# Right half of the up rows as one dense product, left half gathered, down rows first

## The reference

```python
    top_s, pos = lax.top_k(cand, PEER_TOPK)
    idx = jnp.take_along_axis(cand_idx, pos, axis=-1)      # 16 of 16384 experts, for each token and each of 8 heads
    gate = jax.nn.softmax(top_s, axis=-1)
    ...
        u_sel = jnp.take(expert_down, ib, axis=0)           # 128 rows of 2048 for each token
        act = jnp.einsum('tkd,td->tk', u_sel, hb)
        w = gb * jax.nn.gelu(act, approximate=False)
        v_sel = jnp.take(expert_up, ib, axis=0)             # 128 other rows for each token
        return jnp.einsum('tk,tkd->td', w, v_sel)
```

## Time and profile before

| | us |
|---|---|
| median of three runs | 3584.25 (3583.43 to 3586.36) |
| span of the profiled execution | 3584.6 |
| busy in it: PE / POOL / DVE / ACT | 3250.7 / 2185.8 / 1757.3 / 1332.6 |

### The profile page before, as it was taken

One profiled execution on the slowest core, in us unless ns is written; L12 is line 12 of the kernel. 1 busy time (PEld: TensorE's weight loads), 2 busy tenths in 40 slices (PEclk: granted clock), 3 DMA queues, 4 the chain that ended last, 5 costly groups with the idle time before them and its releaser, 6 DMA issues.

```text
span 3584.6 us, 38956 instructions
## 1 busy us (share of the span) xinstructions
PE 3250.7 (91%) x13696; PEld 2311.8 (64%) x13696; DVE 1757.3 (49%) x2582; ACT 1332.6 (37%) x2038; POOL 2185.8 (61%) x1216
## 2 busy tenths in 40 slices
PE   9999999996787788777777789999999999999998
PEld 7888878874343334222322338888888888888887
DVE  8998264238566447544744452222232233335444
ACT  6776576442111011000100014444444444445553
POOL 2021767876445444455455537887788778878665
PEclk9999999998999999999999999999999999999999
DMA  7455545659999999999999985555555455555444
GB/s 230 138 150 139 169 147 164 210 195 367 419 419 420 421 419 421 421 419 421 421 416 422 418 344 194 176 176 170 167 175 174 168 168 176 175 187 174 150 144 170
DMA packets 232766, 936.79 MB, mean 261 GB/s; under 512 B 28177, under 2 KB 31249, under 8 KB 166033
## 3 DMA queue, kind: packets, MB, share of 16 engines
q0 software_dynamic: 76288, 538.74, 36.4%
q1 hardware_dynamic: 152848, 391.96, 33.7%
q10 hardware_dynamic: 3456, 3.77, 0.3%
HBM read 927.04 MB, written 2.10 MB: 259 GB/s over the span
## 4 chain that ended last, share of the span: by engine, by line
PE 65%; DMA 25%; DVE 5%; POOL 2%; issue 1%; DVEq 1%; ACT 1%; ACTq 0%; POOLq 0%
PE products L675 41%; DMA arena<-peer_up_in,arena 22%; PE products L2190 8%; PE products L1545 6%; DMA arena<-peer_down_in,arena 3%; DVE arena L2145 1%; POOL arena L2136 1%; PE products L1215 1%; PE products L2752 1%; PE products L1321 1%; PE products L2714 1%; PE products L1238 1%; POOL weights_low L1480 1%; DVE weights_low L634 1%; DVE arena L2171 0%
## 5 line engine op out<-in xcount | busy, mean ns | idle before, releaser
L634 POOL TENSOR_TENSOR weights_low<-arena,weights_high 128x1024 fp32r<-128x1024 f32 x484 | 1187.5, 2462 | 370.4 <-ACT weights_high L622 324.4
L2190 PE MATMUL products<-arena 128*128 128x512 f32 x1984 | 937.0, 619 | 289.5 <-DMA arena<-peer_up_in,arena 235.5
L622 ACT ACTIVATE weights_high<-arena 128x1024 fp32r<-128x1024 f32 x604 | 637.8, 1059 | 981.0 <-PE products L675 949.3
L675 PE MATMUL products<-weights_high,input_high 128*128 128x512 f32 x2416 | 985.4, 408 | 14.9 <-DVE weights_low L634 13.3
L675 PE MATMUL products<-weights_low,input_high 128*128 128x512 f32 x2416 | 947.2, 392 | 0.0
L675 PE MATMUL products<-weights_high,input_low 128*128 128x512 f32 x2416 | 944.5, 391 | 0.0
L2190 PEld LDWEIGHTS products<-arena 128*128 128x128 f32 x1984 | 370.5, 195 | 838.1 <-issue 416.6
L2145 DVE SCALAR_TENSOR_TENSOR arena<-arena 128x2048 f32<-128x2048 f32 x256 | 585.7, 2292 | 520.6 <-DMA arena<-peer_down_in,arena 520.2
L2136 POOL DMA_INDIRECT arena<-peer_up_in,arena x256 | 391.4, 1529 | 522.8 <-PE products L2190 499.9
L675 PEld LDWEIGHTS products<-weights_high,input_high 128*128 128x128 f32 x2416 | 455.6, 189 | 111.2 <-DVE weights_low L634 15.7
L675 PEld LDWEIGHTS products<-weights_low,input_high 128*128 128x128 f32 x2416 | 454.6, 188 | 98.2
(11 more groups left out here) (369 smaller groups left out, 3088.4 us busy)
## 6 DMA issues: line engine op xcount, KB each, us to landing
arena<-dsa_in SPq DMA_DIRECT2D x320, 512.0 KB, 3.5
arena<-w_in_in SPq DMA_DIRECT2D x128, 512.0 KB, 3.8
arena<-mla_wide_in SPq DMA_DIRECT2D x88, 512.0 KB, 3.5
arena<-w_attn_o_in SPq DMA_DIRECT2D x32, 512.0 KB, 3.8
arena<-w_out_in SPq DMA_DIRECT2D x32, 512.0 KB, 4.7
arena<-peer_w_query_in SPq DMA_DIRECT2D x32, 512.0 KB, 10.2
arena<-dsa_w_out_in SPq DMA_DIRECT2D x32, 512.0 KB, 3.7
arena<-glu_w_b_in SPq DMA_DIRECT2D x16, 512.0 KB, 3.8
```

Of the source, the lines that this page charges most:

```text
L622: nc.scalar.activation(w_hi[:, u % RING, :, at], ring[:, u % RING, :, at], ACT.Copy).then_inc(hi_made, 1)
L634: ops.tensor_tensor(w_lo[:, u % RING, :, at], ring[:, u % RING, :, at], w_hi[:, u % RING, :, at].bitcast(F32), op=ALU.subtract).then_inc(l ...
L675: mm = nc.tensor.matmul(PS[:, bank(b) + t, 0:width], x[:, x0 + n, at], y, start=n == 0 and m == 0, stop=n == len(parts) * PK - 1 and m == 2)
L2190: mm = nc.tensor.matmul(PS[:, SUM_BANKS[q]], diag[:, d % ROWS], row[:, q * NC:(q + 1) * NC], start=h % 2 == 0 and n == 0, stop=bool(last))
```

## The change

- All 256 down rows come first, in eight buffers (`load_down`, `dot_row`). In heads 1 to 12 three of 16 (n = 4, 8, 12: `helped`) are multiplied by POOL in place (`multiply_row`) and summed by ACT (`sum_row`, now another function); DVE dots the rest. POOL multiplies row j - 4 behind the gather of row j.
- Up rows are split by columns into two tensors in main memory, `up_left` and `up_right`, 16384 x 1024 each. The left half is still gathered, 256 gathers of 0.52 MB (`load_half`, six buffers), and added to X by DVE with the weight as a scalar (`add_half`).
- The right half is read whole, 128 chunks of 128 x 1024 (`load_dense` on SP, four buffers), and multiplied on PE by a dense matrix of weights: `spread[t][i2, i1, token]` is the weight of expert i1 x 128 + i2 for a token, zero where it isn't chosen. It is made for four tokens a group, 64 groups: POOL compares i2 with 0..127 for the 128 chosen experts of each token (`mark_keys`), DVE does so with i1 and multiplies by the weight (`mark_weights`), PE multiplies the two one-hot matrices (`spread_group`), ACT copies the result (`take_group`). Groups 0 to 28 stand among the last two heads' rows, the other 35 behind them. `dense_rows` waits for all 64.
- The input of the second block is turned in another order (left half of both tiles, then right half), and SP fills the first weight tiles as buffers come free. The half products between the last rows are gone. Masks and rope tables move behind the middle of the dense product.

```diff
+DOWNS = ROW_HEADS * TOPK
+HALVES = [(4 * r + 2 * t + p, n) for r in range(PEER_H // 2) for p in range(2) for n in range(TOPK) for t in range(NT)]
+HALF_BUFS = 6
+DENSE_BUFS = 4
+GROUP = 4
+LAST_OF_TILE = (13, 15)
+HELPED = (4, 8, 12)
+def helped(h, n):
+    return 1 <= h <= 12 and n in HELPED
+def group_of(h, n):
+    g = (h - LAST_OF_TILE[0]) * TOPK + n - GROUP_SLOT
+    return g if 0 <= g and h < ROW_HEADS - 1 else None
...
+        def multiply_row(pool, j):
+            down_here(pool, j)
+            t = j // TOPK // 2 % 2
+            nc.gpsimd.tensor_tensor(down_place(j), down_place(j), h2[:, t], op=ALU.mult).then_inc(down_multiplied, 1)
+        def sum_row(act, h, n):
...
+            nc.scalar.activation(down_place(j), down_place(j), ACT.Copy, accum_out=acts[:, h % 2, n:n + 1])\
+                .then_inc(down_summed, 1)
...
+        def add_half(dve, m):
...
+            nc.vector.scalar_tensor_tensor(out=X[:, t, 0:HALF], in0=halves[m % HALF_BUFS], scalar=weights[:, t, h // 4, h % 2, n:n + 1],
+                                           in1=X[:, t, 0:HALF], op0=ALU.mult, op1=ALU.add).then_inc(halves_used, 1)
+            if t == NT - 1:
+                dve.drain()
...
+        def mark_keys(pool, g):
...
+            if g >= 2:
+                pool.wait_ge(spread_made, g - 1)
+            for c in range(GROUP):
+                n = GROUP * b + c
+                k = nc.gpsimd.tensor_scalar(hots[:, g % 2, 0, c], iota, picks_t[:, 1, t, n:n + 1], None, ALU.is_equal)
+            k.then_inc(hot_keys, 1)
+        def spread_group(pe, g):
+            pe.wait_ge(hot_keys, g + 1)
+            pe.wait_ge(hot_weights, g + 1)
...
+            for c in range(GROUP):
+                mm = nc.tensor.matmul(PS[:, GROUP_BANKS[g % 4], c * P:(c + 1) * P], hots[:, g % 2, 0, c], hots[:, g % 2, 1, c],
+                                      start=True, stop=True)
+        def dense_rows(pe):
+            pe.wait_ge(spread_read, GROUPS)
+            for i in range(P - DENSE_LAST):
+                for t, q in ((0, 2), (0, 3), (1, 2), (1, 3)):
+                    mm = dense_product(pe, i, t, q, False)
+                mm.then_inc(dense_used, 1)
+                j = i - (P - DENSE_LAST - 4)
+                if j >= 0:
+                    x_turned_pe(pe, j)
+            for t, q in STAGED:
+                for i in range(P - DENSE_LAST, P):
+                    mm = dense_product(pe, i, t, q, i == P - 1)
+                mm.then_inc(dense_made, 1)
...
+            for j in range(DOWNS):
...
+                load_down(pool, j)
...
+                if j >= 4 and helped(*divmod(j - 4, TOPK)):
+                    multiply_row(pool, j - 4)
+                g = j - (LAST_OF_TILE[0] + 1) * TOPK - DOWN_BUFS - 2
+                if g >= 0:
+                    mark_keys(pool, g)
+            for m in range(HALF_BUFS):
+                load_half(pool, m)
+                mark_keys(pool, g + 1 + m)
...
+            for g in range(TILE_GROUPS, GROUPS):
+                mark_keys(pool, g)
+                if g % 2:
+                    load_half(pool, HALF_BUFS + (g - TILE_GROUPS) // 2)
+            for m in range(HALF_BUFS + TILE_GROUPS // 2, len(HALVES)):
+                load_half(pool, m)
...
+            weigh_head(dve, ROW_HEADS - 1)
+            dve.drain()
+            for g in range(FIRST_FREE_GROUP, GROUPS):
+                mark_weights(dve, g)
+                if g >= TILE_GROUPS and g % 2:
+                    add_half(dve, (g - TILE_GROUPS) // 2)
+            for m in range(TILE_GROUPS // 2, len(HALVES)):
+                add_half(dve, m)
```

More of the change, by code:

```diff
@@ L357, in take, with program @@
         return v
-def program(nc, I, out, table, stream, wide, narrow, latent, early, matrices):
+def program(nc, I, out, table, stream, wide, narrow, latent, early, matrices, up_left, up_right):
     ctx = ExitStack()
@@ L2016, in program, with tile_lists @@
         CHOSEN = ((0, 0, 1), (0, 1, 2), (0, 2, 4), (1, 0, 4), (2, 0, 4), (3, 0, 4))
+        def tile_lists(chosen):
+            _, m0, m1 = CHOSEN[chosen]
+            for t in range(NT):
+                first, last = max(m0, 2 * t), min(m1, 2 * t + 2)
+                if first < last:
+                    yield t, slice(first, last), slice(first - 2 * t, last - 2 * t)
         def halve_best(dve, chosen, s, ks):
             V = nc.vector
[L2021 removed]
+            r, m0, m1 = CHOSEN[chosen]
             m, ms, n = m1 - m0, slice(m0, m1), ks.stop - ks.start
@@ L2035, in halve_best @@
             dve.drain()
-            V.tensor_reduce(picked[:, s, ms, ks], hv, AX_X, ALU.add)
+            for t, here, to in tile_lists(chosen):
+                V.tensor_reduce(picks[:, s, t * PEER_H // 2 + r, to, ks], hv[:, here.start - m0:here.stop - m0], AX_X, ALU.add)
             dve.drain()
@@ L2042, in name_experts @@
             ms = slice(m0, m1)
-            nc.vector.scalar_tensor_tensor(out=index_f[:, ms, ks], in0=picked[:, 0, ms, ks], scalar=float(NKEYS),
-                                           in1=picked[:, 1, ms, ks], op0=ALU.mult, op1=ALU.add)
+            for t, here, to in tile_lists(chosen):
+                i1, i2 = (picks[:, s, t * PEER_H // 2 + r, to, ks] for s in range(2))
+                nc.vector.scalar_tensor_tensor(out=index_f[:, here, ks], in0=i1, scalar=float(NKEYS), in1=i2,
+                                               op0=ALU.mult, op1=ALU.add)
             dve.drain()
@@ new lines, in down_place, with down_free, down_here @@
+        def down_place(j):
+            return (up_rows if j % DOWN_BUFS < ROWS else down_rows)[:, j % ROWS]
+        def down_free(eng, j):
+            h, n = divmod(j, TOPK)
+            before = sum(helped(*divmod(i, TOPK)) for i in range(j))
+            if helped(h, n):
+                eng.wait_ge(down_summed, before + 1)
+            else:
+                eng.wait_ge(down_used, j - before + 1)
+        def down_here(eng, j):
+            eng.wait_ge(down_in[j % DOWN_BUFS], 16 * (j // DOWN_BUFS + 1))
@@ new lines, in multiply_row @@
+        def multiply_row(pool, j):
[3 more added lines that the diff above has]
+        def sum_row(act, h, n):
+            j = TOPK * h + n
+            act.wait_ge(down_multiplied, sum(helped(*divmod(i, TOPK)) for i in range(j)) + 1)
+            nc.scalar.activation(down_place(j), down_place(j), ACT.Copy, accum_out=acts[:, h % 2, n:n + 1])\
+                .then_inc(down_summed, 1)
@@ L2140, in dot_row @@
         def dot_row(dve, h, n):
+            if helped(h, n):
+                return
+            j = TOPK * h + n
             t = h // 2 % 2
-            row_here(dve, "down", h, n)
-            row = row_place("down", h, n)
+            down_here(dve, j)
+            row = down_place(j)
             nc.vector.scalar_tensor_tensor(out=row, in0=row, scalar=1.0, in1=h2[:, t],
@@ new lines, in load_dense, with dense_product @@
+        def load_dense(sp, i):
+            if i >= DENSE_BUFS:
+                sp.wait_ge(dense_used, i - DENSE_BUFS + 1)
+            else:
+                down_free(sp, DOWNS - DOWN_BUFS + 2 + i // 2)
+            sp.dma_start(dense[i % DENSE_BUFS], up_right[i * P:(i + 1) * P]).then_inc(dense_in[i % DENSE_BUFS], 16)
+        def dense_product(pe, i, t, q, last):
+            pe.wait_ge(dense_in[i % DENSE_BUFS], 16 * (i // DENSE_BUFS + 1))
+            return nc.tensor.matmul(PS[:, DENSE_BANKS[t, q]], spread[t][:, i],
+                                    dense[i % DENSE_BUFS][:, (q - 2) * NC:(q - 1) * NC], start=i == 0, stop=last)
```

379 lines of the change are left out of this document (209 added, 170 removed).

## The result

The changed kernel took 3829.64 us (median of 4 runs, 3828.61 to 3832.09) beside 3584.7 for the kernel before (four runs; the three of the table above had 3584.25): a ratio of 1.0683, 95% interval 1.0668 to 1.0699, or 245 us slower. The forecast said slower, 3689, and the time lies above its range of 3530 to 3810. The profiled execution spans 3826.8 us for 3584.6, 242 more.

A forecast was written before the change was run, and what follows sets the result against it. The prediction took the 1273 us row stage to be bound by transferred bytes, at 420 GB/s. Its new terms, 668 + 112 + 105 + 490 + 3 = 1378, are 105 more: 3584.25 + 105 = 3689 us, range 3530 to 3810.

The forecast's parts named there:

- heads 1 to 13: Down-row stage: dots, POOL products, choices and splits beside the gathers take 668 us; bounded by transfers alone 518.
- heads 14, 15 with one-hots: Last two heads of down rows, with 29 groups of one-hot matrices: 112 us, 22 rows at 4.5 and 10 at 2.49.
- rest of the spreading: The 35 groups left after the last dot, paced by POOL at 5.8 us per two groups: 105 us.
- dense product: PE's product beside the half gathers: transfers of 463 us at 405 GB/s plus 27 for the last eight chunks, 490.
- into the second layer: PE starts the second layer without the half products that stood in the row stage: 3 us.
- rival 4: One-hot stage dearer, each POOL compare behind a dot or add: second and third terms 77 us more, 3766; chance 0.06.
- plain head: Heads 4, 5, 8, 9, 10, 12: 13 dots, three POOL products, three gathers outside dots, 46.5 us each.
- every gather behind a dot: Upper bound for the six heads 4, 5, 8, 9, 10, 12: 6 x 49.4 = 296 us, against 279 forecast.
- Heads with a choice of four lists: Heads 3, 7, 11, with a choice among their dots: 64 us each, 192 together (bounds 174 and 222).
- Rival 1: Heads 1 to 13 through spreading: POOL's products don't stop dots, compares and gathers fit; 82 us less, 3502; chance 0.2.
- Rival 2: Dense stage: half gathers paced by DVE's adds, 2.34 us each, 575 us for 490, 3774 in all; chance 0.1.
- rival 3: Dense stage: the two streams, halves and chunks, get 358 GB/s together, 3750 us in all; chance 0.04.

## Why the prediction was right and wrong

Most of the mechanisms were right: products and dots take turns, gathers pass one per dot, the transfers nearly stop while the one-hots are made (68 GB/s), and the dense stretch is bound by bytes at about 405 GB/s (402 measured from 1883 to 2353 us). The sign followed from them. The sizes did not: 138 us were missing from the sum of 1378.

| step | forecast (bounds), us | measured, us |
|---|---|---|
| heads 1 to 13 | 668 (518 to 733) | 723 |
| heads 14, 15 with one-hots | 112 (80 to 144) | 166 |
| rest of the spreading | 105 (75 to 150) | 125 |
| dense product | 490 (455 to 545) | 498 |
| into the second layer | 3 | 4 |

- *Heads 14 and 15* (54 of the 138) are the step that failed, and the only one outside its bounds. It failed twice. First the price of a row with comparisons, 4.5 us: the prediction took "0.35 without waits" for a comparison of which it says "no row shows that operation", and "0.5 of waits". The comparison takes 0.60 (590/600 ns in minimum and median), so four are 1.0 us a row dearer; with its waits a row takes 5.56, and 22 rows are 23 us more. Then the path: the sum counted 22 such rows, let the other ten run at the transfers' 2.49 and took off 12 us, as if the dots only followed their gathers. It had no wait of DVE for the one-hots. But the weights between the dots wait for PE, and PE for the comparisons, so the dots kept the comparisons' pace to the last one: POOL's last gather of a down row began at 1722.9 us, the last dot at 1756.1. The other ten rows took 44 us for 13. Leaving out the dots showed that 60 us of this stretch go with POOL and the dots holding each other up. By mechanism it is rival 4 (comparisons behind dots): it had 77 us for this term and the next together, and they missed by 74.
- *Heads 1 to 13* (55). The product's own term held: 4.50 or 3.82 us for 4.65, and in a plain head DVE is busy 39.6 to 42.4 us, for the 42.7 that its dots and three products were to take. Plain heads took 49.4 for 46.5. That is the size of the upper bound, "every gather behind a dot", but not its reading: in head 8 three of the 16 gathers took 0.94 us outside a dot, as in the forecast. DVE waited for rows instead, 5.3 to 9.1 us a head for 3.7: the gathers stand in POOL's queue behind the product and then behind the rest of its dot, the transfers fall behind, and a late row costs DVE's time too. Heads with a choice of four lists were 72 for 64, and they fall to 60 without the product. The forecast allowed 4 us there, for products "that don't fall beside the choice's one-input operations"; they cost some 11, because each of the three held up an operation of DVE. In heads 3, 7 and 11 the first met a dot, the second a cast and the third a product with the gates (L2136, 4.79 for 0.23). The cast has one input, and it takes 0.23 us in the run with the product left out. In head 3 of the changed kernel, in order of time:

```profile
1010.65 4.45 DVE L2107 CAST arena<-arena 128x128 f32<-128x128 uint32 x1
1011.18 3.82 POOL L2176 TENSOR_TENSOR arena<-arena 128x2048 f32<-128x2048 f32 x1
```

  Head 1 was 62 for 53, heads 2 and 6 together 110 for 104.
- *The rest of the spreading* (20): eight comparisons at 5.58 and a gather at 1.01 make 6.8 us per two groups for 5.8, again the price of the comparison. PE lies beside it, as forecast: the eight passes of a group take 2.07 us, though one pass takes 0.43 at the lower clock for the 0.28 assumed.
- *The dense product* (8): 470 us of transfers for 463, and eight chunks behind the last half, as described.

Rival 1 (faster) fell with the first dot of 6.4 us. Rival 2 (halves paced by the adds, each 2.34 us) fell with gathers each 1.99 us, rival 3 (358 GB/s) with the 402 GB/s. The range was too narrow above: the upper ends of the five terms together make 3886 us, and it stopped at 3810, as if one of them at a time could miss. But the first three share one cause, DVE and POOL taking turns, and missed to the same side together.

What stays open: whether another order of the same parts would win. The choices of heads 3, 7 and 11 might be spread over plain heads, where DVE waits 2.3 to 2.9 us for rows in the run without help. By that, seven heads have room for some 18 of the 81 us by which these three exceed the transfers; this was not run. Why a product is cheaper for row 8 than for rows 4 and 12 is open too.

## What to carry to other kernels

A gain in bytes is real only as long as the transfers bound every stretch: before moving work out of a long stage bound by transfers, write down each new stretch with its busiest engine, and expect their limits to add up where the old stage averaged them. Handing a row from VectorE to GpSimd is no help while VectorE's own instruction reads two inputs in SBUF (the on-chip memory) and GpSimd's reads there too. Here it was nearly free beside VectorE's searches (MAX8, FIND_INDEX8), not beside a cast, and GpSimd's gathers stand behind it in either case. An operation without a row in the trace gets its price from the nearest row of its own engine and its bounds widened by the waits of its queue: here the price was 1.7 times the guess. And an engine's fixed order carries a wait further than the engine it began on: follow each new semaphore, here from the comparisons over PE to the dots, before letting rows run at the transfers' pace.

## What the runs showed of the hardware that was not expected

- POOL's multiplication of 128x2048 by a constant took 5.39 us, longer than its product of two such inputs (4.50 or 3.82).
- That product took 4.50 us at least for rows 4 and 12 of a head, which lie in one buffer, and 3.82 at least for row 8, which lies in another. The multiplication by a constant (5.39) and the memset (1.82) showed no such difference; no run tells the buffer from the rest.
- A cast of 128x128 on DVE, one input, took 0.23 us alone and 4.45 beside a product on POOL, ending 0.1 us after it; the searches MAX8 and FIND_INDEX8 kept their durations.
- A gather waits for a TENSOR_TENSOR of two inputs in the on-chip memory as it does for a dot: in the kernel before, the gather of 975.42 us took 1.64 us and ended 0.8 after such a subtraction of DVE (L634); with DVE quiet one takes 0.94.
- Beside a product on POOL a dot ended 2.2 us after it, nearly its whole length; beside the multiplication by a constant 0.42 us after it. So in the second case the dot did most of its work meanwhile; why was not separated.
- The same four comparisons of 128x128 cost 2.38 us on POOL and 0.86 on DVE; one of 128x1024 on DVE, which makes twice as many columns, cost 1.21.
